# The first input projection and the preparation of a recurrence, in one stage instead of two

## What is computed

```python
p = h @ w_cat                                   # h: rms_norm(x), 1024 x 1024
p_rwkv = p_rwkv + (p_prev - p_rwkv) * mu        # p_prev: the token before
r, k, v, z, wd, ad = split(p_rwkv, [512, 1024, 1536, 2048, 2112])
w = -softplus(-(w0 + tanh(wd) @ w_up)) - 0.5
a = sigmoid(a0 + ad @ a_up)
kk = k * k_k;  kk = kk / maximum(sqrt(sum_per_head(kk * kk)), 1e-12)
k = k * (1 + (a - 1) * k_a)
# the scan over tokens takes r, exp(-exp(w)), k, v, -kk, kk * a
bonus = sum_per_head(r * k * r_k) * v
```

## Time and profile before

| | us |
|---|---|
| median of 3 runs | 2632.88 |
| the profiled execution, its own time | 2632.82 |
| its span in the profile | 2631.0 |
| TensorE busy in the span | 2477.4 (94%) |
| VectorE, ScalarE, GpSimd busy | 1116.9, 765.8, 860.9 |

### The profile page before, as it was taken

One profiled execution on the slowest core, in us unless ns is written; L12 is line 12 of the kernel. 1 busy time (PEld: TensorE's weight loads), 2 busy tenths in 40 slices (PEclk: granted clock), 3 DMA queues, 4 the chain that ended last, 5 costly groups with the idle time before them and its releaser, 6 DMA issues. The chain is left out here.

```text
span 2631.0 us, 43685 instructions
## 1 busy us (share of the span) xinstructions
PE 2477.4 (94%) x18356; PEld 1975.6 (75%) x18356; DVE 1116.9 (42%) x1304; ACT 765.8 (29%) x1204; POOL 860.9 (33%) x517
## 2 busy tenths in 40 slices
PE   5996899999999999989899997989989999999999
PEld 4883577777777888868777885767768888887887
DVE  4446322222222244364364455754368667661000
ACT  3222222222212111143252103552354333332210
POOL 0223322122201122234353341125336455555621
PEclk8996999999999999999999998999999999999999
DMA  5116433222203111134423332012322222224431
GB/s 172 48 40 244 118 86 87 82 83 80 83 30 95 41 57 56 49 115 139 148 88 120 81 83 60 25 50 92 113 80 88 96 80 81 79 88 140 150 117 66
DMA packets 257714, 238.72 MB, mean 91 GB/s; under 512 B 35792, under 2 KB 218320, under 8 KB 257296
## 3 DMA queue, kind: packets, MB, share of 16 engines
q1 hardware_dynamic: 251712, 224.80, 27.4%
q10 hardware_dynamic: 5840, 11.54, 1.6%
HBM read 166.80 MB, written 61.90 MB: 87 GB/s over the span
## 5 line engine op out<-in xcount | busy, mean ns | idle before, releaser
L177 POOL TENSOR_TENSOR wlo<-wraw,whi 128x1024 fp32r<-128x1024 f32 x87 | 214.4, 2465 | 699.2 <-ACT whi L172 685.8
L3140 PE MATMUL tl_ps_bank<-tl_dn,tl_hid 128*128 128x512 f32 x1056 | 242.3, 392 | 3.7 <-POOL tl_dn L2840 3.7
L3140 PEld LDWEIGHTS tl_ps_bank<-tl_dn,tl_hid 128*128 128x128 f32 x1056 | 200.0, 189 | 45.9 <-issue 4.1
L981 PE MATMUL rs_ps_bank<-hT_hi,rs_f_hi 128*128 128x512 f32 x384 | 172.1, 448 | 19.3 <-DVE rs_f_out L896 10.3
L172 ACT CAST whi<-wraw 128x1024 fp32r<-128x1024 f32 x87 | 91.3, 1049 | 324.6 <-PE br_ps_ps L199 117.9
L199 PE MATMUL br_ps_ps<-hT_hi,whi 128*128 128x512 f32 x448 | 177.9, 397 | 5.8 <-PEq L107 5.8
L199 PE MATMUL br_ps_ps<-hT_lo,whi 128*128 128x512 f32 x448 | 175.7, 392 | 0.0
L199 PE MATMUL br_ps_ps<-hT_hi,wlo 128*128 128x512 f32 x448 | 175.7, 392 | 0.0
L2678 PE MATMUL tl_ps_bank<-tl_M,tl_ophi 128*128 128x512 f32 x528 | 167.0, 390 | 0.0
L981 PE MATMUL rs_ps_bank<-hT_lo,rs_f_hi 128*128 128x512 f32 x384 | 152.7, 398 | 0.0
L981 PE MATMUL rs_ps_bank<-hT_hi,rs_f_lo 128*128 128x512 f32 x384 | 152.7, 398 | 0.0
(11 more groups left out here) (441 smaller groups left out, 5610.0 us busy)
## 6 DMA issues: line engine op xcount, KB each, us to landing
wraw<-in_w_in SPq DMA_DIRECT2D x79, 512.0 KB, 4.1
scratch_pg<-rs_f_out SPq DMA_DIRECT2D x48, 256.0 KB, 2.4
wraw<-in_w_out SPq DMA_DIRECT2D x24, 512.0 KB, 3.9
tl_raw<-in_w_gate SPq DMA_DIRECT2D x11, 1024.0 KB
tl_raw<-in_w_up SPq DMA_DIRECT2D x11, 1024.0 KB, 5.4
scratch_hid<-tl_H SPq DMA_DIRECT2D x11, 1024.0 KB, 4.9
tl_hidraw<-scratch_hid SPq DMA_DIRECT2D x22, 512.0 KB, 3.3
tl_dnraw<-in_w_down SPq DMA_DIRECT2D x44, 256.0 KB, 2.7
```

Source lines behind the costliest of these rows:

```text
L177: self.nc.gpsimd.tensor_tensor(self.lo[s][:, :], self.raw[s][:, :], self.hi[s][:, :].bitcast(F32), ALU.subtract).then_inc(self.lo_ready, 1)
L981: ins = mm(F[:, h, :], a[:, c], b[:, k, cols[h]], start=k == 0 and u == 0, stop=k == KD - 1 and u == 2)
L3140: ins = nc.tensor.matmul(bank[b][:, :], hid[k][:, x, c], dn[n % 2][:, v, :], start=k == 0 and j == 0, stop=k == FF - 1 and j == 2)
```

## The change

The second function is gone, and its work is interleaved into the first. The 13 tiles go in the order 12, then for each quarter c its key tile (4+c), query tile (c) and value tile (8+c); their positions n are 0, then 1+3c, 2+3c and 3+3c. The token shift is made in halves. The buffers that were double (`run`, `kk`, `b`, `kp`, `a`) are single, the square, root and reciprocal are taken per quarter, and PSUM is four banks for the products, two for `w` and `a`, two for sums, transposes and bonus in turn. The stores are issued per quarter between the weight loads. The first gate tile is loaded at the end of the stage, the second by ACT at the start of the scan. All loops of the stage are written out.

```diff
+    order = [12] + [base + c for c in range(4) for base in (4, 0, 8)]
+    N = len(order)
+    key, query, value = (lambda c: 1 + 3 * c), (lambda c: 2 + 3 * c), (lambda c: 3 + 3 * c)
...
+        bv = d.rms
         ps = [sh.ps(f"ps{n}", [P, HALF]) for n in range(4)]
-        copied, step, shifted = (sh.sem(n) for n in ("copied", "step", "shifted"))
-        mu = d.vec("mu")
+        wa_ps, s_ps = ([sh.ps(f"{n}{h}", [P, HALF]) for h in range(2)] for n in ("wa", "s"))
...
+                def first_stores(c):
+                    sp.wait_ge(run_ready, c + 1)
+                    sp.dma_start(d.rl[:, c, :], run[:, :]).then_inc(run_out, 16)
+                    sp.wait_ge(kp_ready, c + 1)
+                    sp.dma_start(d.rk[:, c, :], kp[:, :]).then_inc(kp_out, 16)
+                    sp.wait_ge(shifted, 2 * query(c) + 2)
+                    sp.dma_start(d.rr[:, c, :], R[:, c, :]).then_inc(kept, 16)
+
+                def second_stores(c):
+                    sp.wait_ge(kk_ready, 2 * c + 2)
+                    sp.dma_start(d.ra[:, c, :], kk[:, :]).then_inc(kk_out, 16)
+                    sp.wait_ge(shifted, 2 * value(c) + 2)
+                    sp.dma_start(d.rv[:, c, :], R[:, 8 + c, :]).then_inc(kept, 16)
+                    sp.wait_ge(b_ready, c + 1)
+                    sp.dma_start(d.rb[:, c, :], b[:, :]).then_inc(b_out, 16)
+
+                def bonus_store(c):
+                    sp.wait_ge(bv_ready, 2 * c + 2)
+                    sp.dma_start(d.rbv[:, c, :], bv[:, :]).then_inc(bv_out, 16)
+                for n in range(N):
+                    t = n + 2
+                    w.load(sp, t, t % 2, rwkv_in_source(d, order[t]) if t < N else following[t - N])
+                    for c in range(4):
+                        if n == value(c):
+                            first_stores(c)
+                        if n == value(c) + 2:
+                            second_stores(c)
+                        if n == value(c) + 3:
+                            bonus_store(c)
...
+                w.wait_split(sp, N)
+                sp.dma_start(w.raw[1][:, :].rearrange("p (k c) -> p k c", k=KD), merge_source(d, 0, 0)).then_inc(gate_in, 16)
+                second_stores(3)
+                bonus_store(3)
...
+                def removal(c):
+                    pool.wait_ge(kk_ready, 2 * c + 2)
+                    if c:
+                        pool.wait_ge(b_out, 16 * c)
+                    nc.gpsimd.tensor_tensor(b[:, :], kk[:, :], a[:, :], ALU.mult).then_inc(b_ready, 1)
+                for n in range(N):
+                    c = at.get(n)
+                    if n and n == query(c):
+                        pool.wait_ge(gain_ready, c + 1)
+                        nc.gpsimd.tensor_tensor(kp[:, :], kp[:, :], R[:, 4 + c, :], ALU.mult).then_inc(kp_ready, 1)
+                    if n == N - 1:
+                        removal(3)
+                    w.split_lo(pool, n + 2, n % 2)
+                    if n and n == value(c) and c < 3:
+                        removal(c)
...
+                def square(c):
+                    act.wait_ge(shifted, 2 * key(c) + 2)
+                    if c:
+                        act.wait_ge(summed, c)
+                    nc.scalar.activation(sq[:, :], R[:, 4 + c, :], ACT.Square, scale=d.vec("kkw", c, c + 1)).then_inc(sq_ready, 1)
...
+                def sigmoids(c, h):
+                    if c:
+                        act.wait_ge(run_ready, c)
+                    else:
+                        act.wait_ge(pads, 1)
+                    act.wait_ge(w_done, 2 * c + h + 1)
+                    nc.scalar.activation(chunks[:, 8 * h:8 * h + 8, 1:PAD], wa_ps[0][:, :].rearrange("p (n c) -> p n c", c=CHUNK),
+                                         ACT.Sigmoid, bias=d.vec("w0", c, c + 1)).then_inc(sig_ready, 1)
+                    if c:
+                        act.wait_ge(gain_ready, c)
+                        act.wait_ge(b_ready, c)
+                    act.wait_ge(a_done, 2 * c + h + 1)
+                    nc.scalar.activation(a[:, half[h]], wa_ps[1][:, :], ACT.Sigmoid, bias=d.vec("a0", c, c + 1)).then_inc(a_ready, 1)
+
...
+                for n in range(N):
+                    c = at.get(n)
+                    if n >= 2:
+                        act.wait_ge(shifted, 2 * n - 2)
                     for h in range(2):
-                        w.wait_product(act, t, h)
-                        nc.scalar.copy(p[u][:, 1 + h * HALF:1 + (h + 1) * HALF], ps[2 * u + h][:, :]).then_inc(copied, 1)
-
-                def tile(t, u, j):
-                    evacuate(t, u)
-                    w.split_hi(act, t + 2, u, j + 1)
-                turns(act, N, tile)
+                        w.wait_product(act, n, h)
+                        nc.scalar.copy(p[n % 2][:, 1 + h * HALF:1 + (h + 1) * HALF], ps[2 * (n % 2) + h][:, :]).then_inc(copied, 1)
+                        if h == 0 and n == key(0):
+                            act.wait_ge(shifted, 2)
+                            nc.scalar.activation(R[0:HEAD, 12, :], R[0:HEAD, 12, :], ACT.Tanh).then_inc(tanh_ready, 1)
+                        if h == 0 and n and n == query(c):
+                            square(c)
+                            sigmoids(c, 1)
+                    w.split_hi(act, n + 2, n % 2, n // 2 + 1)
+                    if n and n == key(c):
+                        sigmoids(c, 0)
+                    if n and n == query(c):
+                        act.wait_ge(summed, c + 1)
+                        nc.scalar.activation(norms(c), stat_ps, ACT.Sqrt).then_inc(root, 1)
...
+                def bonus(c):
+                    if c:
+                        dve.wait_ge(bv_out, 16 * c)
+                    dve.wait_ge(shifted, 2 * value(c) + 2)
+                    for h in range(2):
+                        dve.wait_ge(b_done, 2 * c + h + 1)
+                        nc.vector.tensor_tensor(bv[:, half[h]], b_ps(c)[h][:, :], R[:, 8 + c, half[h]], ALU.mult).then_inc(bv_ready, 1)
...
+                for n in range(N):
+                    c = at.get(n)
+                    if n == value(3):
+                        receptance(3)
+                        direction(3)
+                    shift(n, 0)
+                    if n and n == query(c):
+                        decays(c)
+                        gain(c)
+                        if c:
+                            bonus(c - 1)
+                    if n and n == value(c) and c < 3:
+                        receptance(c)
+                    shift(n, 1)
+                    if n and n == query(c):
+                        norm(c)
+                    if n and n == value(c) and c < 3:
+                        direction(c)
+                bonus(3)
...
+                def low_rank(c, h):
+                    cols = slice(c * P, (c + 1) * P)
+                    for lo, bank, done in ((0, wa_ps[0], w_done), (HEAD, wa_ps[1], a_done)):
+                        nc.tensor.matmul(bank[:, :], up[lo:lo + HEAD, cols], R[lo:lo + HEAD, 12, half[h]], start=True, stop=True).then_inc(done, 1)
+
+                def bonus(c):
+                    pe.wait_ge(rkr_ready, c + 1)
+                    if c == 3:
+                        pe.wait_ge(a_ready, 8)
+                    else:
+                        pe.wait_ge(kk_ready, 2 * c + 2)
+                    for h in range(2):
+                        nc.tensor.matmul(b_ps(c)[h][:, :], d.blockones[:, :], rkr[:, half[h]], start=True, stop=True).then_inc(b_done, 1)
+
+                def back(c):
+                    pe.wait_ge(widened, c + 1)
+                    turn_back(nc, s_ps, wide, d.ident).then_inc(returned, 1)
+
+                for n in range(N):
+                    c = at.get(n)
+                    w.wait_split(pe, n)
+                    for h in range(2):
+                        if n >= 2:
+                            pe.wait_ge(copied, 2 * n - 3 + h)
+                        for k in range(KD):
+                            ins = half_products(nc, w, ps[2 * (n % 2) + h], w.slot(n % 2), hT, k, half[h])
+                        ins.then_inc(w.product, 1)
+                        if h == 0 and n and n == query(c):
+                            pe.wait_ge(sig_ready, 2 * c + 1)
+                            pe.wait_ge(a_ready, 2 * c + 1)
+                            low_rank(c, 1)
+                        if h == 0 and n == value(3):
+                            back(3)
+                    if n and n == key(c):
+                        if c:
+                            pe.wait_ge(a_ready, 2 * c)
+                        else:
+                            pe.wait_ge(loaded, 48)
+                            pe.wait_ge(tanh_ready, 1)
+                        low_rank(c, 0)
+                        if c:
+                            bonus(c - 1)
+                    if n and n == query(c):
+                        pe.wait_ge(sq_ready, c + 1)
+                        if c:
+                            pe.wait_ge(bv_ready, 2 * c)
```

(10 more changed lines are left out.)

215 lines of the change are left out of this document (60 added, 155 removed).

## The result

The changed kernel took 2591.43 us (median of 4 runs, 2588.1 to 2595.38) against 2633.41 for the kernel before on the same chip: ratio 0.9845, 95% interval [0.9825, 0.9866]. Run again under the name `after_again` it took 2591.11 (0.9854 [0.9838, 0.987]). The forecast was 2595.7, the range 2590 to 2610. The profiled execution took 2588.1 us, its span is 2586.0, and its mean clock is 0.98.

What follows compares the result with a forecast made beforehand. TensorE was taken to bound the projection, with 72.6 us between its last product and the scan's first transfer removable: 72.6 - 23.7 (insertions) - 1.5 (waits) - 9.3 (tail) - 1.0 (scan start) = 37.1 us less, 2595.7 us; range 2590 to 2610.

Steps and rivals of the forecast that it cites:

- Low-rank products: Two side-by-side matmuls for `w` and `a` per half tile, now between products: 0.9 us a half, eight halves 7.2 us.
- Bonus sums: TensorE's four records of 512 columns per quarter: 1.71 us a round, three rounds before the last product, 5.1 us.
- returns: Going back to products: the first record after inserted work takes 0.09 us more, 16 times, 1.4 us.
- Sums of squares: TensorE's 16 records per quarter between products: 1.70 us a round, four rounds 6.8 us.
- PE waits 0.5 us for VectorE's bonus, three times: Ahead of the sums of quarters 1 to 3, PE waits for VectorE's bonus to leave their bank: 1.5 us in all.
- slower by this half: Every step of VectorE's chain slowed by half beside POOL: PE waits 3 us more each time; no chance of its own.
- The tail: From the last product's end to the scan's first transfer: copy, mix, bonus, hand-overs and stores, 9.3 us.
- The scan's start: ACT's load of the second gate tile beside SP's first loads delays VectorE and PE's recurrence: 0 to 1.9 us, taken as 1.0.
- the rule that was weighed: At the scan's start, transfers issued from different engines share the same 16 DMA engines, making the delay the full 1.9 us.
- the clock falls at the sums: Rival: narrow sums behind a wait lower PE's clock, 2.4 us lost in products and 0.9 in sums, four times; 2609, chance 0.08.
- PE waits for the chain: Rival: VectorE's pace shows in every quarter of the stage, 4 x 4.6 = 18 us; 2614, chance 0.08.
- The slower case: Rival: the clock falls at all 16 insertions between products, 61 us; 2656, slower than before, chance 0.04.

Runs made afterwards that it cites:

- unrolled_pe: The kernel before with only TensorE's loop over the 13 tiles of the first projection written out; 2624.93 us, ratio 0.9971 to the kernel before.
- bonus_late: The changed kernel with VectorE's bonus product moved behind the second half of the query tile's mix; 2617.61 us, ratio 0.9946 to the kernel before.
- gate_late: The changed kernel with both gate weight loads issued after the first four of SP's row transfers are in, behind the first gate tile's split; 2590.82 us.
- split_first: The changed kernel with ScalarE splitting the first gate tile before it issues its load at the scan's start; 2593.74 us, ratio 0.9856 to the kernel before.
- unrolled_rest: The kernel before with the first projection's loops of SyncE, GpSimd, ScalarE and VectorE written out, TensorE's kept; 2631.74 us, ratio 1.0004 to the kernel before.
- sums_twice: The changed kernel with TensorE making every quarter's sums of squares twice over; 2605.06 us, ratio 0.9902 to the kernel before.
- gain_thrice: The changed kernel with VectorE computing the gain three times over ahead of its bonus product in each quarter; 2602.24 us, ratio 0.9886 to the kernel before.

## Why the prediction was right, and where it was not

The direction, the size and the mechanism were right. The 77 us gap closed to 16.5 and came back as 27 us of insertions. The sum was right partly by luck: the part that it describes gave less than forecast, and a part that it did not know of gave the rest. From the stage's first product to the scan's transposes the two profiles before took 236.1 and 236.3 us, the two after 202.1 and 203.0: 33.7 us gained, where 37.1 were forecast. Behind that, from the transposes to the end, the same profiles give 11.8 us more. (The profiled executions of the changed kernel lie 2 to 3 us below its medians, which differ from the kernel before by 42.0 us and not by 45.) `unrolled_pe` reaches 8.9 of the 11.8 with no other edit (2343.7 - 2334.8), at some 1 us lost in its stage. Variants of the changed kernel scatter from 2331.5 to 2338.5 there, so 5 to 12 us is what can be said.

Point by point:

- **Low-rank products, 0.9 a half.** Mis-sized: an insertion of one half alone adds 1.26, with its return, where 0.99 was said. The estimate took two pairs of 0.43 and let the rest of the first start count as drain. The row it came from, 244.16 to 246.16 for both halves, read as it stands gives 1.0 a half, or 1.09 with the return. Another 0.09 is the way in, which was not counted: the first low-rank record starts 0.32 us behind the last product's start, where a product would start 0.227 behind it. Eight halves: 2.2 us.
- **Bonus sums 1.71, transposes 0.79, returns 0.09.** Right: transposes add 0.88, as said. Low-rank and bonus together add 2.98, where 2.70 was said (0.9, 1.71 and one return), and the difference is the low-rank term.
- **Sums of squares 1.70 a round.** Right: 1.80 with the return, where 1.79 was said. The rows of the later projection carried over to another stage to 0.01 us.
- **PE waits 0.5 us for VectorE's bonus, three times.** It waits 0.2 to 0.3. The chain was given 1.1 us for the mix of half a tile, "half of 2.17, POOL being idle then". POOL is idle there in the changed kernel, but it was not at the row that the 2.17 came from: GpSimd's product beside it ran until 250.33, 1.1 us into it. The changed trace shows half a tile alone at 0.75, and `bonus_late` shows it ending when GpSimd does, so that 2.17 was in part a wait in disguise. The rival built on it ("slower by this half") had the wrong form too, since the price is no factor. It depends on where GpSimd's operation stands, up to 2 us at a time.
- **The tail, 9.3.** 8.5. The last mix took 0.75, not 1.6: it began 0.27 us ahead of GpSimd's split and did not wait for it.
- **The scan's start, 1.0 of at most 1.9.** From SP's first transfer to the transposes it took 21.1 and 21.8 instead of 20.2 and 20.5, 1.0 more as forecast, but by luck: the forecast had the transposes wait for VectorE, whose `rs_bt` came only 0.5 us later than before in the mean (21.0 and 20.6 against 20.2 and 20.5), and the rest is TensorE's own gate products behind ScalarE's long issue. VectorE's first copy was promised at about 15 us and came at 14.6 and 14.9. (Against the two kernels with the old stage and PE's loop written out, 13.6 and 13.8, that is 1.0 us later.) The full 1.9 by the rule that was weighed did not come. But in `gate_late`, where the megabyte is issued later and beside SP's last rows, the copy came another 1.3 later. That the ScalarE queue would stand for 3.3 us at one issue was not foreseen. The first 2 us of it went into the gate tile's slack, and the remainder showed: `split_first` takes the issue out of the way, and TensorE waits for VectorE again.
- **The opening.** Not in the sum: the first 8 products run at half clock in the profile of before and the first 14 in both of after, which is 1.2 us of the 3.4 missing. Other kernels with the changed stage had 9 to 14, and `unrolled_rest`, with PE's loop kept, had 13, so this is scatter at least in part.
- **What changes downstream: nothing.** This was the step left out. The forecast put the later stages at nothing without a reason, and they gave 5 to 12 us.

Together: low-rank +2.2, waits and tail -1.6, opening +1.2, one quarter at half clock in one profile of two +0.7. Against 3.4 us missing that leaves about 1 unexplained, within the scatter of edges.

**The rivals.** That the clock falls at the sums was given 0.08 with 2609. Its mechanism was shown to be real and near. It takes one more round (`sums_twice`, 2605) or 1.5 us more of waiting (`gain_thrice`, 2602), and where it came it cost 1.4 to 2.1 us a quarter in products and up to 2.0 in the sums (`bonus_late`: 9.79 less the wait of 5.9 and the 1.80), where the forecast had 2.4 and 0.9. That PE waits for the chain was given 2614 with 0.08, and `bonus_late` makes it true by moving one VectorE operation: 2618. The two rivals were kept apart in the forecast, yet they act together: a wait ahead of the sums lets the clock fall, and 5 us of waiting cost 14 of stage. (The clock can also fall behind two rounds of sums with 0.2 us of waiting.) The slower case, the clock falling at all 16 insertions, came nowhere near: low-rank, bonus and transposes left the products at full speed in every trace.

## What to carry to other kernels

Small fp32 matmuls put between full products cost PE their own time, within 0.3 us of the rows elsewhere in the same kernel, and nearly nothing else, as long as PE comes to them without waiting. A wait of 1.75 us ahead of narrow matmuls was paid nearly three times over in the stage (14 us for 5), because the clock went with it. So in such an interleaving put first on the helper engine what TensorE waits for next, even where the profile shows only 0.2 us of waiting. And an edit that moves TensorE's later program can change the time of stages far behind it: measure the edit's own stretch in the trace, and count 0.3% of the total as possible luck of placement.

## What the runs showed of the hardware that was not expected

- Writing out one loop of TensorE's is worth 7.3 us (ratio 0.9971 [0.996, 0.9982]), most of it over 900 us behind the loop, with the same instructions executed apart from the loop's own. The load of `i_sin` took 6.4 to 6.5 us with a packet of the instruction queue q8 in flight, and 4.5 to 4.8 without. Writing out the other four engines' loops did nothing (1.0004 [0.9992, 1.0016]).
- A VectorE mix with two inputs in SBUF takes 0.75 us for 512 columns alone, and ends 0.55 us behind a GpSimd operation that was running (2.80 and 2.85 us). Durations of such operations in a trace are therefore not to be taken for theirs until GpSimd's timeline has been laid beside them.
- The clock did not fall at once behind narrow work, but 1.0 to 1.3 us into the products behind it (`after_again`, the second quarter of `sums_twice`), for some 3 us. Behind a wait of 1.75 us it fell within the sums, behind 5.9 us before they began.
- A DMA issue on ScalarE's queue took 3.15 to 3.48 us in eight traces where it came 1.2 us behind SP's first row transfer, and 0.47 us when it came at 5.0 (`gate_late`). The single one of the kernel before, 1.0 us behind SP's first, took 0.49. What makes it long is not settled: a packet of a second instruction queue, q14, moves within it in all eight and in none of the short ones, but in the changed trace two other issues of ScalarE's with such a packet took 0.61 each.
